# The last matrix product of a two-layer forward pass in wide groups with seven products for eight

## The chip, the cores and the metric

One core of a Trainium2 chip runs the kernel. The metric is the device time of one execution in microseconds: before, the median of 3 runs is 1776.52 us (1776.01 to 1777.11).

## The reference

256 tokens of width 2048 in float32 pass through two layers. The first is softmax attention with a forget-gate bias and a squared-ReLU MLP, each between norms. The second is a hybrid layer: a norm, one wide projection, block attention beside a gated spatial mix, two projections, and their gated sum. The change touches only its last line:

```python
    merged = jax.nn.sigmoid(g_a) * y_a + jax.nn.sigmoid(g_b) * y_b
    return x + merged @ w_out
```

`merged` is 256x2048 and `w_out` is 2048x2048.

## The kernel before

**Products.** Every float32 matrix is split into a high part (rounded to the type fp32r) and a low part (the rest), and a product of two blocks is three matmuls: high by high, low by high, high by low. A product here has 128 tokens (t = 0 or 1), a slice of 128 features of the input (kt, 0 to 15) and 512 output columns, and adds into one PSUM bank.

**The stream.** All weights come from one tensor `stream` in chunks of 128x1024 values. SP loads chunk c into slot c % 4 of `raw` (L393 to L395, and the loop at L432 to L436); it may do so once the low part of chunk c - 4 is made. ScalarE copies it to `w_hi` (L987, `split`/`next_split`), once TensorE is done with chunk c - 4 (`chunk_done`). VectorE makes `w_lo` = `raw` - `w_hi` (L1516, `rest`), which signals `lo_ready`, for which TensorE waits. `next_split(k)` and `rest(k, slot)` make the parts of chunk k + 4. Each engine runs its instructions in the order in which its block of the program lists them; that order is written by hand.

**Narrow groups.** The output phase (`FIRST["out"]`, 32 chunks) has four groups of 512 columns. A chunk of a narrow group holds two slices kt of its 512 columns, so 2 x 2 x 3 = 12 matmuls (`group_chunk`, L462). Groups alternate between two pairs of banks (2, 3 and 4, 5); at a group's end VectorE adds the residual rows to each bank (L2298) into `group_sum`, and SP stores that block (L441).

**Wide groups.** The MLP's second matrix and the q, k, v projection are done in groups of 1024 columns and 16 chunks. A chunk is one slice kt of 1024 columns: 2 token halves by 2 column blocks, 12 matmuls too (`wide_chunk`, L775). Three pairs of chunks (`SEVEN_AT`, chunks 4, 8 and 12, with the kt pairs 4, 5 and 6) are instead a 2x2 by 2x2 block product with seven products in place of eight, 21 matmuls (`seven_products`, L789; matmuls at L768 to L770). It needs:
- of x: four combinations of the four 128x128 blocks (`h_forms` on VectorE, L2041: two additions of high and low part, then four additions or subtractions), their high part on ScalarE (L1325) and low part on VectorE (`h_forms_lo`, L2064), once for all groups that share x
- of the weights, for each step: four 512-column additions or subtractions on VectorE (`outer_sums`, `inner_sum`, `last_sum`, L1866 to L1879), a 1536-column high part on ScalarE (`wide_form`, L1242) and low part on VectorE (`form_rest`, L1885)
- at the end: four banks of seven-products (`seven`) beside four banks of plain sums (`plain`). ScalarE copies `seven[0]` to SBUF (L1256), VectorE joins the others to it in four additions (`join_seven`, L1915 to L1924), and adds the plain banks in four more once the group is done (`plain_drain`, L1896).

One `wide_step` (VectorE) is: outer sums, inner sum, last sum, low part of two chunks, `form_rest`, low part of two chunks. In a group that follows another, the four drains of the group before are put between its sums.

**Around the output phase.** The projection `proj_a` has four groups. After its group n VectorE makes 512 columns of the merged matrix (L2276, L2282); TensorE turns them with eight transposes into banks 6 and 7 (`turn_merged`, L953) two to three chunks later; ScalarE makes the high part (`merged_to_hi`, L1491) and VectorE the low part (`merged_to_lo`, L2262), which counts `merged_ready` up by one for each kt, 16 in all. The last quarter, kt 12 to 15, is turned after the third chunk of the output phase. Before each chunk j of the first narrow group TensorE waits for `merged_ready` 2j + 2.

Of the kernel before, what the change touches and what calls it, by code (L numbers as in the profile page):

```python
# [43 lines left out]
QKV_WIDE = 3  # L44
EPS = 1e-6
# [52 lines left out]
def build(nc, stream, x, x_turned, fox_w_f, fox_b_f, norm_rows, norm_cols, w_spatial, b_spatial, head_cols, out):  # L98
    fox_scratch = nc.dram_tensor("cum_rows", (FOX_HEADS, TOK), F32, kind="Internal").ap()

    with ExitStack() as ctx:
# [90 lines left out]
        def in_a(name, at, shape, dt=F32R):  # L192
# [8 lines left out]
                          in_a("h_x_hi", 4608, [STEPS, 4, P]), in_a("h_x_lo", 6144, [STEPS, 4, P]), h_part)  # L201
        hidden = [gate_flat[:, b * 256:(b + 1) * 256] for b in range(2)]
# [22 lines left out]
        h_bank = [[bank[2], bank[3], bank[7], bank[6]], [bank[0], bank[1], bank[5], bank[4]]]  # L225
        h_seven = [[bank[0], bank[4], bank[1], bank[5]], [bank[2], bank[6], bank[3], bank[7]]]
# [165 lines left out]
        def _(sp):  # L392
# [44 lines left out]
            for n in range(4):  # L437
                for t in range(NT):
                    sp.wait_ge(out_ready, n * NT + t + 1)
                    cols_n = slice(n * GROUP_COLS, (n + 1) * GROUP_COLS)  # L440
                    sp.dma_start(out[0, t * P:(t + 1) * P, cols_n], group_sum[:, t, cols_n]).then_inc(stored, 16)  # L441
# [4 lines left out]
        def _(pe):  # L446
# [328 lines left out]
            def wide_chunk(c, j, kt, plain, x, bank_free={}):  # L775
# [3 lines left out]
                for t in range(NT):  # L779
                    for n in range(2):  # L780
                        if first and 2 * t + n in bank_free:
                            bank_free[2 * t + n]()
                        x_block = [part[:, kt, t * P:(t + 1) * P] for part in x]
                        mm = product(plain[2 * t + n], x_block, w_block(j % RING, n), first, last)
                    if last and t == 0:
                        mm.then_inc(half_group_done, 1)
# [185 lines left out]
            def merged_in(j):  # L972
                return lambda: pe.wait_ge(merged_ready, 2 * j + 2)
# [8 lines left out]
        def _(act):  # L982
# [261 lines left out]
            def wide_split(c, w, j, forms, seven):  # L1244
# [7 lines left out]
                if j == SEVEN_AT[-1] + 1:  # L1252
                    act.wait_ge(forms_done, STEPS * w + STEPS)
                    if 0 < w < WIDE_GROUPS:
                        act.wait_ge(added[0][0], 16 * w)
                    nc.scalar.activation(forms.part[0], seven[0][:, :], ACT.Copy).then_inc(form_hi_ready, 1)  # L1256
# [65 lines left out]
            def h_forms_hi(q):  # L1322

                act.wait_ge(x_form_step, 4 * STEPS * FF_GROUPS + 6 * q + 6)
# [187 lines left out]
        def _(dve):  # L1512
# [528 lines left out]
            def h_forms(q):  # L2041

                done = 4 * STEPS * FF_GROUPS + 6 * q
# [17 lines left out]
            def h_forms_lo(q):  # L2061

                dve.wait_ge(x_form_hi_ready, STEPS * FF_GROUPS + q + 1)
# [222 lines left out]
            for n in range(4):  # L2286
                cols_n = slice(n * GROUP_COLS, (n + 1) * GROUP_COLS)
                for j in range(8):
                    if 8 * n + j < 32 - RING:
                        rest(c + 8 * n + j, j % RING)  # L2290
                    if n == 0 and j == 2:
                        merged_to_lo(3)
                for t in range(NT):
                    if t == 0:
                        dve.wait_ge(half_group_done, GROUPS_BEFORE["out"] + n + 1)
                    else:
                        dve.wait_ge(chunk_done, c + 8 * n + 8)
# [253 lines left out]
```

## Time and profile before

| | us |
|---|---|
| median of 3 runs | 1776.52 |
| the profiled execution's own time | 1777.32 |
| its span in the trace | 1775.6 |
| TensorE busy | 1766.9 |
| VectorE busy | 1278.1 |
| ScalarE busy | 895.5 |

The trace is of one execution; its times count from the start of the span. PE is TensorE, DVE VectorE, ACT ScalarE. A line of a timeline merges like instructions that follow each other: start, time to the end of the last, how many. Matmuls overlap, so a matmul's own duration (0.39 us) is longer than the distance to the next.

### The profile page before, as it was taken

Reading aid. Unit: us, or ns where it says so; the run is one execution under the profiler, and the core shown is the slowest. Engines: PE = TensorE matmul, PEld = TensorE weight load, DVE = VectorE, ACT = ScalarE, POOL = GpSimd, SP = SyncE. Lnnn points to the kernel's source line nnn. Section 1 sums busy time; section 2 is a strip of 40 time slices with the busy share of each in tenths; the row PEclk is TensorE's granted clock in tenths of the full one; section 3 lists DMA queues with packets and bytes.
Section 4 is the critical chain, followed back from the end, with each engine's and each line's share of the span. In section 5 each row is a group of like instructions: output and inputs, shape, how many; then the busy total and the mean of one; then the engine's idle time right before and its main releaser. Section 6 shows DMA issues by size and latency. Waiting matters only on the chain.

```text
span 1775.6 us, 26289 instructions
## 1 busy us (share of the span) xinstructions
PE 1766.9 (100%) x8791; PEld 1496.7 (84%) x8791; DVE 1278.1 (72%) x1689; ACT 895.5 (50%) x1248; POOL 139.4 (8%) x190
## 2 busy tenths in 40 slices
PE   9999999999999999999999999999999999999999
PEld 7888888888888888888888887788888888888887
DVE  6567777556788788778887877899788655555654
ACT  7434444446456445545554455757644445553442
POOL 1012122000001000100000000010013011000000
PEclk9999999999999999999999999999999999999999
DMA  9664455555567666865785676566655655555554
GB/s 330 196 224 161 161 164 167 189 177 190 167 215 229 197 191 210 227 201 191 214 236 190 196 228 216 177 203 202 198 184 175 200 178 178 177 175 187 183 190 154
DMA packets 99116, 347.30 MB, mean 196 GB/s; under 512 B 11472, under 2 KB 11872, under 8 KB 98656
## 3 DMA queue, kind: packets, MB, share of 16 engines
q1 hardware_dynamic: 93392, 333.23, 57.3%
q0 software_dynamic: 4784, 12.60, 3.4%
q8 instruction: 50, 0.82, 0.2%
q10 hardware_dynamic: 864, 0.44, 0.1%
q14 instruction: 26, 0.21, 0.0%
HBM read 336.77 MB, written 2.11 MB: 191 GB/s over the span
## 4 chain that ended last, share of the span: by engine, by line
PE 94%; DVE 3%; ACT 1%; DMA 1%; issue 1%; POOL 0%; SPq 0%; ACTq 0%; DVEq 0%
PE bank L474 32%; PE bank L453 23%; PE bank L458 12%; PE bank L768 7%; PE bank L769 7%; PE bank L770 7%; PE bank L490 1%; PE bank L524 1%; DMA raw<-in_stream 1%; DVE w_lo L1516 1%; PE bank L603 1%; PE bank L646 1%; PE bank L661 1%; ACT w_hi L987 1%; PE bank L652 0%
## 5 line engine op out<-in xcount | busy, mean ns | idle before, releaser
L1516 DVE TENSOR_TENSOR w_lo<-raw,w_hi 128x1024 fp32r<-128x1024 f32 x620 | 753.9, 1224 | 372.1 <-ACT w_hi L987 368.1
L987 ACT ACTIVATE w_hi<-raw 128x1024 fp32r<-128x1024 f32 x620 | 648.3, 1055 | 583.8 <-PE bank L474 267.1
L453 PE MATMUL bank<-h_both,w_hi 128*128 128x512 f32 x1792 | 432.6, 393 | 0.0
L453 PEld LDWEIGHTS bank<-h_both,w_hi 128*128 128x128 f32 x1792 | 330.4, 188 | 65.4
L474 PE MATMUL bank<-w_hi,h_both 128*128 128x512 f32 x1160 | 361.6, 393 | 0.0
L474 PEld LDWEIGHTS bank<-w_hi,h_both 128*128 128x128 f32 x1160 | 215.8, 188 | 43.5
L458 PEld LDWEIGHTS bank<-h_both,w_lo 128*128 128x128 f32 x1792 | 229.8, 191 | 8.7
L458 PE MATMUL bank<-h_both,w_lo 128*128 128x256 f32 x1792 | 232.5, 283 | 0.0
L474 PE MATMUL bank<-w_lo,h_both 128*128 128x512 f32 x580 | 226.1, 390 | 0.0
L474 PE MATMUL bank<-w_hi,a_both 128*128 128x512 f32 x576 | 178.5, 391 | 0.0
L474 PEld LDWEIGHTS bank<-w_lo,h_both 128*128 128x128 f32 x580 | 108.9, 188 | 23.0
L474 PEld LDWEIGHTS bank<-w_hi,a_both 128*128 128x128 f32 x576 | 107.5, 188 | 21.9
L768 PE MATMUL bank<-w_hi,a_both 128*128 128x512 f32 x322 | 125.5, 390 | 0.2 <-DVE w_lo L1516 0.2
L769 PE MATMUL bank<-w_hi,a_both 128*128 128x512 f32 x322 | 125.3, 389 | 0.0
L770 PE MATMUL bank<-w_lo,a_both 128*128 128x512 f32 x322 | 125.3, 389 | 0.0
L474 PE MATMUL bank<-w_lo,a_both 128*128 128x512 f32 x288 | 112.2, 389 | 0.0
L1225 ACT ACTIVATE a_both<-gate 128x256 fp32r<-128x256 f32 (+1 forms) x56 | 23.4, 418 | 139.8 <-DVE gate L1818 139.8
L768 PEld LDWEIGHTS bank<-w_hi,a_both 128*128 128x128 f32 x322 | 60.5, 188 | 13.3 <-issue 0.8
L770 PEld LDWEIGHTS bank<-w_lo,a_both 128*128 128x128 f32 x322 | 60.4, 188 | 12.5
L769 PEld LDWEIGHTS bank<-w_hi,a_both 128*128 128x128 f32 x322 | 60.5, 188 | 12.3
L474 PEld LDWEIGHTS bank<-w_lo,a_both 128*128 128x128 f32 x288 | 54.1, 188 | 11.3
L2395 POOL DMA_DIRECT2D wide<-scaled x21 | 18.4, 1000 | 539.6 <-ACT scaled L1272 539.6
(278 smaller groups left out, 1784.9 us busy)
## 6 DMA issues: line engine op xcount, KB each, us to landing
raw<-in_stream SPq DMA_DIRECT2D x622, 512.0 KB, 3.5
wide<-scaled POOLq DMA_DIRECT2D x21, 256.0 KB, 4.7
res<-in_x SPq DMA_DIRECT2D x4, 512.0 KB, 7.1
rowg<-in_norm_rows POOLq DMA_DIRECT2D x2, 1024.0 KB, 8.3
gate<-cum_rows POOLq DMA_DIRECT2D x1, 2048.0 KB, 8.0
out<-wide SPq DMA_DIRECT2D x8, 256.0 KB, 3.6
wide<-gate POOLq DMA_DIRECT2D x7, 256.0 KB, 8.3
gate<-in_x_turned SPq DMA_DIRECT2D x5, 256.0 KB, 6.7
```

Of the source, the lines that this page charges most:

```text
L453: pe.matmul(tile_sum[b][:, :], w_hi[:, slot + half, k * P:(k + 1) * P], h_both[:, 8 * half + k, :], start=half == 0 and k == 0, stop=False)
L458: mm = pe.matmul(tile_sum[b][:, 0:TOK], w_lo[:, slot + half, k * P:(k + 1) * P], h_both[:, 8 * half + k, 0:TOK], start=False, stop=half == ...
L474: mm = pe.matmul(dst[t][:, :], xt[:, k0 + 2 * j + k, tt], wt[:, slot, w], start=j == 0 and k == 0 and n == 0, stop=last and k == 1 and n == 2)
L490: mm = pe.matmul(dst[t][:, :], xt[:, 2 * j + k, tt], wt[:, slot, w], start=j == 0 and k == 0 and n == 0, stop=j == GROUP_CHUNKS - 1 and k ...
L524: mm = pe.matmul(group_bank[0][t][:, :], xt[:, 2 * j + k, t * P:(t + 1) * P], wt[:, j % RING, w], start=first, stop=False)
L768: pe.matmul(dst[:, :], x_parts[0], w_parts[0], start=start, stop=False)
L769: pe.matmul(dst[:, :], x_parts[1], w_parts[0], start=False, stop=False)
L770: return pe.matmul(dst[:, :], x_parts[0], w_parts[1], start=False, stop=stop)
L987: nc.scalar.activation(w_hi[:, slot, :], raw[:, slot, :], ACT.Copy).then_inc(hi_ready, 1)
L1225: nc.scalar.activation(one(a_hi, i * 2 + b), relu2[b], ACT.Copy).then_inc(ff_hi, 1)
L1516: nc.vector.tensor_tensor(w_lo[:, slot, :], raw[:, slot, :], w_hi[:, slot, :].bitcast(F32), ALU.subtract).then_inc(lo_ready, 1)
L2395: pool.dma_start(group_sum[:, t, start:start + GROUP_COLS], src, accum_op=ALU.add).then_inc(added[t][n], 16)
```

## The change

The output phase becomes two wide groups of 1024 columns, each with three steps of seven products. The weights are laid out in the stream for that. It uses the forms' memory of the q, k, v phase (the weights' raw forms lie elsewhere). The forms of x are made again, of the merged matrix, at the start of the phase. The residual rows are added to the joined parts in SBUF (`add_rows`) and the drains add the plain banks. In the last chunk TensorE also signals when its third of four products is done, so that each drain of the second token half has its own signal, and the eight stores follow the drains.

```diff
+OUT_WIDE = 2
...
+        out_forms = qkv_forms._replace(w_raw=gate_flat[:, 6144:7680].rearrange("p (f n) -> p f n", f=3))
...
+        out_bank = [bank[2:6], [bank[0], bank[6], bank[7], bank[1]]]
+        out_seven = [[bank[0], bank[1], bank[6], bank[7]], [bank[2], bank[5], bank[3], bank[4]]]
...
-            pe.wait_ge(gate_taken[0], 9)
-            group_pair(FIRST["out"], 7, h_hi, h_lo, before={j: merged_in(j) for j in range(8)},
-                       after={2: lambda: turn_merged(3)})
-            group_pair(FIRST["out"] + 16, 8, h_hi, h_lo)
+            def out_group(i):
+
+                c = FIRST["out"] + 16 * i
+                w = WIDE_GROUPS + QKV_WIDE + i
+                if i:
+                    joined(w - 1)
+                else:
+                    pe.wait_ge(gate_taken[0], 9)
+                for j in range(0, WIDE_CHUNKS, 2):
+                    pair = PAIR_ORDER[j // 2]
+                    if i == 0:
+                        pe.wait_ge(merged_ready, 2 * pair + 2)
+                    if j in SEVEN_AT:
+                        if i:
+                            pe.wait_ge(out_ready, 4)
+                        else:
+                            pe.wait_ge(gate_taken[1], 9)
+                            pe.wait_ge(merged_ready, 16)
+                        seven_products(c, j, SEVEN_AT.index(j), w, out_bank[i], out_seven[i], (h_hi, h_lo), out_forms,
+                                       STEPS * (FF_GROUPS + 1))
+                        continue
+                    for k in range(2):
+                        wide_chunk(c, j + k, 2 * pair + k, out_bank[i], (h_hi, h_lo),
+                                   {3: fifth_read(w - 1)} if i else {}, i == OUT_WIDE - 1)
+                        if i == 0 and j + k == 2:
+                            turn_merged(3)
...
-            for k in range(32 - RING):
-                next_split(c + k)
-                if k == 2:
-                    merged_to_hi(3)
+            w = WIDE_GROUPS + QKV_WIDE
+            h_forms_hi(0, 1)
+            wide_split(c, w, 0, out_forms, out_seven[0])
+            h_forms_hi(1, 1)
+            wide_split(c, w, 1, out_forms, out_seven[0])
+            wide_split(c, w, 2, out_forms, out_seven[0])
+            merged_to_hi(3)
+            wide_split(c, w, 3, out_forms, out_seven[0])
+            h_forms_hi(2, 1)
+            for j in range(4, WIDE_CHUNKS):
+                wide_split(c, w, j, out_forms, out_seven[0])
+            for j in range(WIDE_CHUNKS - RING):
+                wide_split(c + 16, w + 1, j, out_forms, out_seven[1])
+            first_part(w + 1, out_forms, out_seven[1])
...
+            def add_rows(i):
+
+                dve.wait_ge(join_step, 8 * (w + i) + 4)
+                for block in range(4):
+                    t, n = divmod(block, 2)
+                    nc.vector.tensor_tensor(h_part[block], h_part[block], res[:, t, out_block(i, t, n)],
+                                            ALU.add).then_inc(join_step, 1)
...
+            step = STEPS * w
+            h_forms(0, 1)
+            outer_sums(step, c + 4, 0, out_forms)
+            inner_sum(step, 0, out_forms)
+            last_sum(step, 0, out_forms)
+            h_forms(1, 1)
+            rest(c, 0)
+            rest(c + 1, 1)
+            form_rest(step, out_forms)
+            h_forms_lo(0, 1)
+            h_forms_lo(1, 1)
+            rest(c + 2, 2)
+            merged_to_lo(3)
+            rest(c + 3, 3)
+            h_forms(2, 1)
+            wide_step(c, w, 1, out_forms)
+            h_forms_lo(2, 1)
+            wide_step(c, w, 2, out_forms)
+            rests(c + 12, range(2))
+            join_seven(w, out_seven[0], h_part)
+            rests(c + 12, range(2, RING))
+            add_rows(0)
+            for q in range(STEPS):
+                if q < STEPS - 1:
+                    wide_step(c + 16, w + 1, q, out_forms, (lambda t, n: out_drain(0, t, n)) if q == 0 else None)
+                else:
+                    outer_sums(step + 5, c + 28, 0, out_forms)
+                    inner_sum(step + 5, 0, out_forms)
+                    last_sum(step + 5, 0, out_forms)
+                    rests(c + 24, range(2))
+                    form_rest(step + 5, out_forms)
+                    rests(c + 24, range(2, RING))
+            join_seven(w + 1, out_seven[1], h_part)
+            add_rows(1)
+            for t in range(NT):
+                for n in range(2):
+                    out_drain(1, t, n)
```

`out_drain(i, t, n)` waits for its half group or last chunk and for its row addition, then writes `group_sum` = `h_part[block]` + bank and counts `out_ready` up; SP stores block by block on that count.

## Rows read from the trace of the kernel before

**Rows 1.** Page: busy time of each engine, and the slices' granted clock (tenths).
```profile
PE 1766.9 (100%) x8791; PEld 1496.7 (84%) x8791; DVE 1278.1 (72%) x1689; ACT 895.5 (50%) x1248; POOL 139.4 (8%) x190
...
PEclk9999999999999999999999999999999999999999
```

**Rows 2.** Chain that ended last, from 1600 us: start us, us, what.
```profile
1681.28 10.90 PE bank L474 x48
1692.18 0.87 PE bank L953 x8
1693.05 78.94 PE bank L474 x348
...
1772.02 0.69 DVE wide L2298
```

**Rows 3.** TensorE's waits: engine line <- releaser: us in total, times, longest.
```profile
PE bank L517 <- POOL ident L2309: 1.7, 1, 1.7
PE bank L768 <- DVE h_w_lo L1885: 1.3, 1, 1.3
```

**Rows 4.** Timeline of VectorE before the output phase: start us, us, engine, line, what.
```profile
1682.67 1.41 DVE L2262 SCALAR_TENSOR_TENSOR h_both<-bank,h_both 128x256 fp32r<-128x256 f32 x4
1685.14 1.23 DVE L1516 TENSOR_TENSOR w_lo<-raw,w_hi 128x1024 fp32r<-128x1024 f32 x1 [1.06 <-ACT w_hi L987]
1686.29 1.28 DVE L2276 SCALAR_TENSOR_TENSOR wide<-gate,bank 128x512 f32<-128x512 f32 x2
1687.71 1.29 DVE L2282 TENSOR_TENSOR wide<-wide 128x512 f32<-128x512 f32 x2
1688.92 1.22 DVE L1516 TENSOR_TENSOR w_lo<-raw,w_hi 128x1024 fp32r<-128x1024 f32 x1
```

**Rows 5.** Timeline of VectorE, forms of x in the q, k, v phase.
```profile
1123.45 1.06 DVE L2059 TENSOR_TENSOR gate<-gate 128x128 f32<-128x128 f32 x1
...
1125.57 0.75 DVE L2048 TENSOR_TENSOR gate<-h_both 128x256 f32<-128x256 f32 x2
...
1127.29 1.22 DVE L1516 TENSOR_TENSOR w_lo<-raw,w_hi 128x1024 fp32r<-128x1024 f32 x1
...
1131.68 1.89 DVE L2064 TENSOR_TENSOR h_x_lo<-gate,h_x_hi 128x512 fp32r<-128x512 f32 x3
```

**Rows 6.** Timeline of VectorE, third wide group of q, k, v.
```profile
1247.36 0.68 DVE L1866 TENSOR_TENSOR h_w_raw<-raw 128x512 f32<-128x512 f32 x1
...
1250.01 2.36 DVE L1516 TENSOR_TENSOR w_lo<-raw,w_hi 128x1024 fp32r<-128x1024 f32 x2
1252.28 1.75 DVE L1885 TENSOR_TENSOR h_w_lo<-h_w_raw,h_w_hi 128x1536 fp32r<-128x1536 f32 x1
1253.95 1.22 DVE L1516 TENSOR_TENSOR w_lo<-raw,w_hi 128x1024 fp32r<-128x1024 f32 x1
...
1260.71 0.69 DVE L1915 TENSOR_TENSOR gate<-gate,bank 128x512 f32<-128x512 f32 x1 [0.35 <-ACT gate L1256]
...
1262.76 0.68 DVE L1924 TENSOR_TENSOR gate<-gate,bank 128x512 f32<-128x512 f32 x1
...
1267.75 2.47 DVE L1896 TENSOR_TENSOR gate<-gate,bank 128x512 f32<-128x512 f32 x4
```

**Rows 7.** Timeline of ScalarE, the same group and the output phase.
```profile
1248.67 2.01 ACT L987 ACTIVATE w_hi<-raw 128x1024 fp32r<-128x1024 f32 x2 [1.11 <-DVE raw L1867]
1250.59 1.48 ACT L1242 ACTIVATE h_w_hi<-h_w_raw 128x1536 fp32r<-128x1536 f32 x1
...
1260.08 0.60 ACT L1256 ACTIVATE gate<-bank 128x512 f32<-128x512 f32 x1 [0.98 <-PE bank L770]
...
1693.18 1.19 ACT L1491 ACTIVATE h_both<-bank 128x256 fp32r<-128x256 f32 x4
```

**Rows 8.** Stores of the output (issues at L441): landing times.
```profile
DMA to landing us min/median/max: 2.4/3.6/5.3
```

**Rows 9.** Timeline of TensorE, the opening's transposes.
```profile
1.67 3.65 PE L517 MATMUL bank<-ident 128*128 128x128 f32 x19 [1.67 <-POOL ident L2309]
```

More of the change, by code:

```diff
@@ L436, in _ @@
                     load(j * RING + slot, slot)
-            for n in range(4):
+            for i in range(OUT_WIDE):
                 for t in range(NT):
-                    sp.wait_ge(out_ready, n * NT + t + 1)
-                    cols_n = slice(n * GROUP_COLS, (n + 1) * GROUP_COLS)
-                    sp.dma_start(out[0, t * P:(t + 1) * P, cols_n], group_sum[:, t, cols_n]).then_inc(stored, 16)
+                    for k in range(2):
+                        n = 2 * i + k
+                        sp.wait_ge(out_ready, 4 * i + 2 * t + k + 1)
+                        cols_n = slice(n * GROUP_COLS, (n + 1) * GROUP_COLS)
+                        sp.dma_start(out[0, t * P:(t + 1) * P, cols_n], group_sum[:, t, cols_n]).then_inc(stored, 16)
             sp.wait_ge(stored, 16 * 4 * NT)
@@ L784, in wide_chunk @@
                         mm = product(plain[2 * t + n], x_block, w_block(j % RING, n), first, last)
+                        if last and final and (t, n) == (1, 0):
+                            mm.then_inc(half_group_done, 1)
                     if last and t == 0:
@@ L1252, in wide_split, with first_part @@
                 if j == SEVEN_AT[-1] + 1:
[L1253 to L1256, printed above, removed]
+                    first_part(w, forms, seven)
+            def first_part(w, forms, seven):
+                act.wait_ge(forms_done, STEPS * w + STEPS)
+                if 0 < w < WIDE_GROUPS:
+                    act.wait_ge(added[0][0], 16 * w)
+                if w == WIDE_GROUPS + QKV_WIDE + 1:
+                    act.wait_ge(out_ready, 4)
+                nc.scalar.activation(forms.part[0], seven[0][:, :], ACT.Copy).then_inc(form_hi_ready, 1)
             def wide_splits(g, n):
@@ L2040, in _, with h_forms @@
             c = FIRST["qkv"]
-            def h_forms(q):
-                done = 4 * STEPS * FF_GROUPS + 6 * q
+            def h_forms(q, lap=0):
+                done = 4 * STEPS * FF_GROUPS + 6 * (STEPS * lap + q)
+                if lap:
+                    dve.wait_ge(merged_ready, 2 * SEVEN_PAIRS[q] + 2)
                 if q:
@@ L2285, in _ @@
             c = FIRST["out"]
[L2286 to L2297, printed above, removed]
-                    nc.vector.tensor_tensor(group_sum[:, t, cols_n], group_bank[n % 2][t][:, :],
-                                            res[:, t, cols_n], ALU.add).then_inc(out_ready, 1)
-                dve.wait_ge(out_ready, 2 * n + 2)
-                dve.sem_inc(group_taken[n % 2], 1)
+            w = WIDE_GROUPS + QKV_WIDE
@@ new lines, in out_block @@
+            def out_block(i, t, n):
+                start = i * 1024 + n * GROUP_COLS
+                return slice(start, start + GROUP_COLS)
+            def add_rows(i):
[4 more added lines that the diff above has]
+                                            ALU.add).then_inc(join_step, 1)
@@ new lines, in out_drain @@
+            def out_drain(i, t, n):
+                block = 2 * t + n
+                if t == 0:
+                    dve.wait_ge(half_group_done, GROUPS_BEFORE["out"] + i + 1)
+                elif i == 1 and n == 0:
+                    dve.wait_ge(half_group_done, GROUPS_BEFORE["out"] + 3)
+                else:
+                    dve.wait_ge(chunk_done, c + 16 * i + WIDE_CHUNKS)
+                dve.wait_ge(join_step, 8 * (w + i) + block + 5)
+                nc.vector.tensor_tensor(group_sum[:, t, out_block(i, t, n)], h_part[block], out_bank[i][block][:, :],
+                                        ALU.add).then_inc(out_ready, 1)
```

19 lines of the change are left out of this document (11 added, 8 removed).

## The prediction

> **What bounds the kernel now.** I read the page first: TensorE is busy for the whole span and the granted clock stands at 9 or more in every slice [rows 1]. The chain of waits says the same of the end: one run of matmuls, with eight transposes between, reaches 1771.99 us, then one VectorE addition of 0.69 us and the last store [rows 2]. The list of TensorE's waits is led by a 1.7 us start and one wait of 1.3 us [rows 3]. So a product less is time less, as long as TensorE stays fed, and any wait put on TensorE is time more. 348 matmuls take 78.94 us [rows 2], 0.227 us each; 12 of them, one chunk, 2.72 us. The output phase starts 36 matmuls and 8.2 us before 1692.18, about 1684.0. About 0.2% (3.6 us) is what a measurement of this kernel can tell from no change.
>
> **Products removed.** Each of two groups has three steps in which 21 matmuls replace 24: 18 fewer, 18 x 0.227 = **-4.1 us**. The stream's bytes and the transposes stay as they are.
>
> **A new wait at the start of the phase.** The first step (chunks 4 and 5) writes banks 0, 1, 6 and 7. Banks 6 and 7 hold the turned last quarter of the merged matrix until VectorE has made its low part, so TensorE waits for merged_ready 16 there. Before, only the eighth chunk of the phase needed that count. TensorE reaches the step after chunk 3, at 1693.05 + 2.72 = 1695.8. I walk VectorE's queue up to the instruction it waits for. VectorE ends the last merging additions at about 1688.9, when it starts the next low part now [rows 4]. In the changed order it then has, by starts of consecutive rows:
> - two sums and four combinations of pair 4: 1127.29 - 1125.57 = 1.72 [rows 5]
> - four weight combinations: 1250.01 - 1247.36 = 2.65 [rows 6]
> - the same six for pair 5: 1.72
> - low parts of chunks 4 and 5: 2 x 1.14, from 2.27 for two [rows 6]
> - the low part of the three weight forms: 1.67 [rows 6]
> - two low parts of the x forms: 1.2, from 1.89 for three [rows 5]
> - low part of chunk 6: 1.14
> - the four low parts of the merged quarter: 1.41 [rows 4].
>
> That is 13.8 us. ScalarE adds to it, because its queue too is in order: the high part of chunk 5 stands behind the high part of pair 5's form, which waits for VectorE until 1694.9, so at 1.0 us for a chunk (2.01 for two [rows 7]) VectorE idles 0.6; the three forms' high part (1.48) follows, another 0.2. ScalarE's four high parts of the quarter (1.19 [rows 7]) are done near 1700.0 and hold nobody. Sum 14.6: VectorE delivers at 1703.5, and TensorE stands for about **7.8 us** (+7.8, counted from its last matmul's issue, 0.1 more than from its modelled end). All of it is bare, since nothing else runs on TensorE. Bounds: 7.0 without ScalarE's part, 9.0 with one stumble such as the 1.06 us that one 128-column combination took where the others took 0.28 [rows 5].
>
> **The rest of the phase.** TensorE has 318 matmuls left, 72.1 us, so its end would be 1703.5 + 72.1 = 1775.6 by issue, 1775.8 by modelled end. VectorE must keep up with twice its old load. Per group: 16 low parts (18.2), three times four combinations and a form (13.0), four joins (2.7), four row additions (2.4), four drains (2.4), 38.7 us against TensorE's 8 x 5.44 - 3 x 0.68 = 41.5. The first group adds 2.3 for pair 6. Walked in order, VectorE's form for the third step is done at 1723.5 for a need at 1726.6, and that of the second group's first step at 1747.9 for a need at 1747.7: a wait of 0.1 or 0.2. The projection of q, k and v runs the same steps, and its one wait was 1.3 us at the phase's first step [rows 3]. I take 0, bounds 0 and 1.3. SP's stream loads are issued when a low part is done, so they go late with VectorE; the four-slot ring leaves 3 us or more between landing and use in my walk, so 0.
>
> **Row additions and tail.** The residual rows leave the last drain and become four additions of their own, after the join. No row shows one; the nearest is an SBUF-only addition of the same size, 1.29 us for two [rows 4], and a drain that reads PSUM, 2.47 for four [rows 6]: 0.60 to 0.65 each. In group 0 they are hidden behind TensorE. In the last group they are not. The last step ends 24 matmuls before the end, at 1770.4; ScalarE's copy takes 0.60 [rows 7], to 1771.0; the four joins 2.7 [rows 6], to 1773.7; four row additions 2.4, to 1776.1; four drains, all behind them in the queue, 2.5, to 1778.6. So VectorE ends 2.8 us behind TensorE where it now ends 0.7 behind: **+2.1**, bounds 1.6 and 3.0. If the row additions were on another engine, the drains would end at about 1776.5 and the tail cost nothing.
>
> **Stores.** The same eight stores, but the last four now come 0.6 us apart instead of the last two six matmuls (1.4 us) apart. Now 2.9 us pass from the last addition to the span's end; landings are 2.4 to 5.3 [rows 8]. I take **+0.2**, bounds 0 and 1.0.
>
> **The clock after the stand.** Nothing in this trace idles TensorE for more than 1.7 us [rows 3], so no row shows what 7.8 us do. The nearest is the opening: TensorE comes out of idle and makes 19 transposes in 3.65 us, 0.192 each [rows 9], where eight of the same size later take 0.87, 0.109 each [rows 2]. By that pace it started at the lower level, 1.2 GHz. That cost 19 x 0.083 = 1.6 us. After a stand four times as long as any here I expect the same, and 512-column products lose more each than transposes do: I take **+2.0**, bounds 0 (the rival below) and 3.2, twice the opening.
>
> A row and a page part here. The granted clock reads full in every slice, the opening too [rows 1], though the transposes there run slow; by that row alone the sum would lack the 2.0. The Trainium skill, "TensorE: Matmul & The Clock Gate", section "Why this matters for your kernels", says that idle gaps between bursts of matmuls put the clock back to its lower level; by it the sum keeps a clock term. No run here shows that yet.
>
> **Sum.** -4.1 + 7.8 + 0 + 2.1 + 0.2 + 2.0 = +8.0 us on the profiled execution (span 1775.6, time 1777.32, which is 0.8 above the median). A difference carries over: 1776.52 + 8.0 = **1784.5**.
>
> **Rivals.**
> 1. *The stand without the clock.* TensorE stays at the upper level; 1784.5 - 2.0 = 1782.5. For it: the granted clock never moves in this trace. Against: the slow transposes of the opening.
> 2. *VectorE becomes the bound after the stand as well.* It starts the rest late and has some 81 us of work in the 90 us from 1688.9 to its end; if three of the five remaining steps each wait 1.3 us, as the one in the q, k, v phase [rows 3], 3.9 more: 1788.4. Against: that phase ran two whole groups with the same queue and no wait, though without the row additions.
> 3. *Not slower: the stand does not form.* The place is the wait for merged_ready 16 at chunk 4. If VectorE came to the quarter's low part before 1695.8, 7.8 and 2.0 fall away: 1774.7, 0.1% under before and within what can't be told. It decides at 1.8 us: a shorter stand gives a gain, a longer one a loss (-4.1 + 2.1 + 0.2 = -1.8). Against it: that low part is behind 12 us of VectorE work which can't begin before 1688.9. For it only that I have misread the order of a queue. That the products are not saved can't be: their number is fixed in the code.
>
> **Chances.** Forecast 0.62, rival 1 0.24, rival 2 0.07, rival 3 0.07. The range: low end with the stand at 7.0, the tail at 1.8 and no clock term, -4.1 + 7.0 + 1.8 + 0.1 = 4.8, 1781.3; high end with the clock at 3.2, tail and stand a little long, near 1788.0. It leaves out rivals 2 and 3 and little more. Faster by over 0.2% needs rival 3 and a hidden tail: 0.02. Within 0.2%: the rest of rival 3 and a little: 0.06. Slower: 0.92.
>
> **What would show it.** In the changed profile TensorE's waits should have one long entry near 1695, about 7.8 us, released by VectorE's low part of the merged quarter (the scalar_tensor_tensor from the bank), and VectorE in one block from 1688.9 to 1703.5 with two small gaps left by ScalarE. Instructions: 18 matmuls fewer. Matmul starts just after the stand should be about 0.43 us apart (512 columns at 1.2 GHz) rather than 0.227 if the clock fell; with rival 1 they are 0.227 at once. At the end VectorE should run 12 additions without a gap of note and finish 2.8 us after the last matmul. The forecast is wrong if the stand is under 5 us or absent, if later steps wait more than 1.5 us in all, or if the tail is as short as now.

## The result, and the profile after

| | us |
|---|---|
| before, median of 5 (1776.01 to 1777.11) | 1776.52 |
| after, median of 5 (1785.96 to 1787.08) | 1786.66 |
| forecast | 1784.5 (1781.3 to 1788.0) |

The ratio is 1.0056 (95% interval 1.0045 to 1.0068): 10.1 us slower, where 8.0 were forecast. The profiled execution has a span of 1785.4 us against 1775.6, a difference of 9.8, and that is what the rows below add up to.

The page's first lines and its row of granted clock:

```profile
span 1785.4 us, 26353 instructions
...
PE 1765.9 (99%) x8773; PEld 1495.9 (84%) x8773; DVE 1318.3 (74%) x1756; ACT 906.3 (51%) x1259; POOL 140.6 (8%) x190
...
PEclk9999999999999999999999999999999999999989
```

18 matmuls fewer than in [rows 1], as the code says, and one dent in the row of nines: the 39th of 40 slices, 1696 to 1741 us, in which the output phase starts. A slice is 44.6 us long and a 9 stands for 90% or more, so this row shows 10 us at half the clock and would hide 3 us. TensorE's waits (engine, line <- releaser: us in total, times, longest):

```profile
PE bank L774 <- DVE h_both L2310: 8.0, 1, 8.0
PE bank L523 <- POOL ident L2406: 1.7, 1, 1.7
PE bank L774 <- DVE h_w_lo L1931: 1.4, 1, 1.4
```

The last two stood there before [rows 3]. The first is new, alone, and 8.0 us long; what released it is the low part of the merged quarter. VectorE's timeline shows the queue that the prediction walked:

```profile
1687.29 1.30 DVE L2330 TENSOR_TENSOR wide<-wide 128x512 f32<-128x512 f32 x2
1688.51 0.75 DVE L2096 TENSOR_TENSOR gate<-h_both 128x256 f32<-128x256 f32 x2
...
1690.23 0.68 DVE L1912 TENSOR_TENSOR gate<-raw 128x512 f32<-128x512 f32 x1
...
1692.89 0.75 DVE L2096 TENSOR_TENSOR gate<-h_both 128x256 f32<-128x256 f32 x2
...
1694.61 1.22 DVE L1562 TENSOR_TENSOR w_lo<-raw,w_hi 128x1024 fp32r<-128x1024 f32 x1
1696.34 1.23 DVE L1562 TENSOR_TENSOR w_lo<-raw,w_hi 128x1024 fp32r<-128x1024 f32 x1 [0.51 <-ACT w_hi L1017]
1697.71 1.76 DVE L1931 TENSOR_TENSOR h_w_lo<-gate,h_w_hi 128x1536 fp32r<-128x1536 f32 x1
1699.39 1.28 DVE L2112 TENSOR_TENSOR h_x_lo<-gate,h_x_hi 128x512 fp32r<-128x512 f32 x2
1700.59 1.22 DVE L1562 TENSOR_TENSOR w_lo<-raw,w_hi 128x1024 fp32r<-128x1024 f32 x1
1701.72 1.41 DVE L2310 SCALAR_TENSOR_TENSOR h_both<-bank,h_both 128x256 fp32r<-128x256 f32 x4
```

From the merging additions (1687.29, 0.4 us earlier than in [rows 4]) to the quarter's low part at 1701.72 there is one gap, 0.51 us at chunk 5, behind ScalarE, and 0.2 more before 1697.71. TensorE over the same time, its last matmul before and the first after the stand:

```profile
1695.02 0.39 PE L776 MATMUL bank<-w_lo,h_both 128*128 128x512 f32 x1
1703.39 0.76 PE L774 MATMUL bank<-w_hi,h_both 128*128 128x512 f32 x1 [7.99 <-DVE h_both L2310]
1703.95 0.63 PE L775 MATMUL bank<-w_hi,h_both 128*128 128x512 f32 x1
1704.38 0.63 PE L776 MATMUL bank<-w_lo,h_both 128*128 128x512 f32 x1
...
1708.64 0.47 PE L774 MATMUL bank<-h_w_hi,h_x_hi 128*128 128x512 f32 x1
1708.95 0.40 PE L775 MATMUL bank<-h_w_hi,h_x_lo 128*128 128x512 f32 x1
```

The first interval is 0.56 us, the eleven behind it are 0.43 each, the last, from 1708.64, is 0.31; then the products are 0.23 apart again. The windows of the timeline give the granted clock beside it (columns: the stretch, its length, busy time and count of TensorE's matmuls, of its weight loads, of VectorE, ScalarE and GpSimd, then the granted clock, the DMA share and GB/s):

```profile
1684.00:1695.00 11.00, 11.00 (x54) 9.17 (x53) 9.92 (x22) 2.66 (x4) 0.00 (x0) 1.00 0.22 82
1695.00:1703.00 8.00, 0.40 (x2) 0.00 (x0) 7.34 (x10) 5.66 (x9) 0.00 (x0) 0.72 0.38 131
1703.00:1709.00 6.00, 5.61 (x14) 4.43 (x15) 5.86 (x13) 1.80 (x3) 0.00 (x0) 0.52 0.53 178
1709.00:1715.00 6.00, 6.00 (x28) 4.98 (x27) 3.98 (x4) 3.50 (x3) 0.00 (x0) 1.00 0.48 175
```

0.52 from 1703 to 1709: TensorE runs at 1.2 GHz, the lower of its two levels. It had stood idle since 1695.4 (the last matmul before, 1695.02 + 0.39); from 1709 on it is back at 2.4 GHz (1.00). The end, VectorE:

```profile
1769.32 2.35 DVE L1562 TENSOR_TENSOR w_lo<-raw,w_hi 128x1024 fp32r<-128x1024 f32 x2
1773.72 0.69 DVE L1961 TENSOR_TENSOR gate<-gate,bank 128x512 f32<-128x512 f32 x1 [2.06 <-ACT gate L1292]
...
1776.49 2.50 DVE L2346 TENSOR_TENSOR gate<-gate,res 128x512 f32<-128x512 f32 x4
1778.90 2.47 DVE L2359 TENSOR_TENSOR wide<-gate,bank 128x512 f32<-128x512 f32 x4
```

and TensorE's last matmul:

```profile
1778.11 0.39 PE L776 MATMUL bank<-w_lo,h_both 128*128 128x512 f32 x1
```

TensorE ends at 1778.11 + 0.39 = 1778.50. VectorE waits for ScalarE's copy until 1773.72 and then has twelve additions without a pause, to 1778.90 + 2.47 = 1781.37, which is 2.87 behind TensorE; before it was 0.7 [rows 2]. From there to the end of the span are 4.0 us, before 2.9.

So the difference of the spans, in microseconds, by rows:

| | forecast | measured |
|---|---|---|
| the stream up to the output phase | 0 | -0.4 |
| 18 products | -4.1 | -4.1 |
| the stand at chunk 4 | +7.8 | +8.0 |
| 13 slow intervals after the stand: 1708.95 - 1703.39 = 5.56, less 13 x 0.227 | +2.0 | +2.6 |
| the rest of the phase | 0 | +0.4 |
| VectorE behind TensorE at the end | +2.1 | +2.1 |
| from the last addition to the end | +0.2 | +1.1 |
| sum | +8.0 | +9.8 (rounded terms give 9.7) |

The -4.1 is the count times the price of one product, as in the forecast; no row measures it alone. The 0.4 in the rest of the phase is what is left when TensorE's end, 6.5 us later than before, is set against the other terms. By the distances of its matmuls, 0.15 of it lies at the edge of the stand (8.14 us of extra distance for 7.99 in the brackets). The prediction counted its 7.8 from the last matmul's issue, which is the 8.14; by that way of counting the rest of the phase is 0.2. That 0.2 lies at 1747.3 to 1747.6, at the first step of group 1, where I had foreseen 0.1 to 0.2 and took none.

### The profile page after: what moved, and what is told of

It is laid out like the page before. It is cut to its first block, busy times and chain, and to the rows that moved or that the text cites. A ratio compares the mean times of both kernels' runs of the same rounds, so it can differ in the third digit from the quotient of the medians.

```text
span 1785.4 us, 26353 instructions
## 1 busy us (share of the span) xinstructions
PE 1765.9 (99%) x8773; PEld 1495.9 (84%) x8773; DVE 1318.3 (74%) x1756; ACT 906.3 (51%) x1259; POOL 140.6 (8%) x190
## 4 chain that ended last, share of the span: by engine, by line
PE 93%; DVE 3%; ACT 2%; issue 1%; DMA 1%; POOL 0%; DVEq 0%; ACTq 0%; SPq 0%; POOLq 0%
PE bank L480 25%; PE bank L459 23%; PE bank L464 12%; PE bank L774 9%; PE bank L776 9%; PE bank L775 9%; PE bank L530 1%; PE bank L496 1%; DVE w_lo L1562 1%; ACT w_hi L1017 1%; DMA raw<-in_stream 1%; PE bank L609 1%; PE bank L652 1%; PE bank L667 1%; PE bank L658 0%
## 5 line engine op out<-in xcount | busy, mean ns | idle before, releaser
L480 PE MATMUL bank<-w_hi,h_both 128*128 128x512 f32 x904 | 282.6, 394 | 0.0
L480 PEld LDWEIGHTS bank<-w_hi,h_both 128*128 128x128 f32 x904 | 167.8, 188 | 33.6
L480 PE MATMUL bank<-w_lo,h_both 128*128 128x512 f32 x452 | 176.3, 390 | 0.0
L480 PEld LDWEIGHTS bank<-w_hi,a_both 128*128 128x128 f32 x576 | 107.4, 188 | 22.4 <-DVE w_lo L1562 0.6
L480 PEld LDWEIGHTS bank<-w_lo,h_both 128*128 128x128 f32 x452 | 84.8, 188 | 18.0
L774 PE MATMUL bank<-w_hi,h_both 128*128 128x512 f32 x230 | 90.4, 393 | 8.4 <-DVE h_both L2310 8.0
L776 PE MATMUL bank<-w_lo,h_both 128*128 128x512 f32 x230 | 90.0, 391 | 0.0
L775 PE MATMUL bank<-w_hi,h_both 128*128 128x512 f32 x230 | 90.0, 391 | 0.0
L774 PEld LDWEIGHTS bank<-w_hi,a_both 128*128 128x128 f32 x322 | 60.4, 188 | 12.7 <-issue 0.3
L776 PEld LDWEIGHTS bank<-w_lo,a_both 128*128 128x128 f32 x322 | 60.5, 188 | 12.6
```

Of the source, the lines that this page charges most:

```text
L480: mm = pe.matmul(dst[t][:, :], xt[:, k0 + 2 * j + k, tt], wt[:, slot, w], start=j == 0 and k == 0 and n == 0, stop=last and k == 1 and n == 2)
L774: pe.matmul(dst[:, :], x_parts[0], w_parts[0], start=start, stop=False)
L775: pe.matmul(dst[:, :], x_parts[1], w_parts[0], start=False, stop=False)
L776: return pe.matmul(dst[:, :], x_parts[0], w_parts[1], start=False, stop=stop)
```

## The experiments

My theory: four separate costs, each with its own place (VectorE's queue at chunk 4; the clock that falls during that stand; VectorE's queue behind the last step; the stores), against 4.1 us of saved products. The rivals: the step itself makes TensorE slow; VectorE's added work is too much wherever it is put; the stores alone set the end.

One table for all kernels helps to read what follows. "TensorE's part" is from the start of the last eight transposes (1692.02 before) to the last matmul's start; "VectorE behind" is the end of the last addition less the end of the last matmul; "stores" from there to the end of the span. The kernel before was run again beside each batch of experiments; its row gives the range of its medians.

| kernel | time, median | TensorE's part | VectorE behind | stores |
|---|---|---|---|---|
| before | 1776.52 to 1776.72 | 79.57 | 0.7 | 2.9 |
| after | 1786.66 | 86.51 | 2.9 | 4.0 |
| e1_fill | 1784.27 | 83.89 | 2.9 | 4.0 |
| e2_norows | 1784.65 | 85.88 | 1.15 | 4.0 |
| e3_order | 1780.73 | 80.39 | 2.9 | 4.0 |
| e4_five_steps | 1778.97 | 78.76 | 2.9 | 4.0 |
| e5_five_reordered | 1777.09 | 76.65 | 2.9 | 4.0 |
| e6_four_steps | 1775.76 | 77.33 | 1.2 | 4.0 |
| e7_two_queues | 1786.17 | 86.80 | 2.9 | 4.0 |
| e8_four_steps_blocks | 1774.30 | 77.30 | 0.7 | 2.9 |
| e9_no_steps | 1776.49 | 79.57 | 0.7 | 2.9 |

**e1_fill: is it the idle time that makes the products slow?**

```diff
                             pe.wait_ge(gate_taken[1], 9)
+                            for _ in range(33 if j == 4 else 0):
+                                pe.matmul(bank[0][:, :], h_hi[:, 0, 0:P], h_both[:, 0, :], start=True, stop=True)
                             pe.wait_ge(merged_ready, 16)
```

> The changed kernel, with 33 dummy matmuls of 512 columns (7.5 us) into the still unused bank 0 ahead of TensorE's wait for merged_ready 16; nothing of the real work is changed. My theory: the 12 products after the stand run 0.427 us apart because TensorE was idle before them, at the lower of its two levels. With the dummies there is no idle time, the products are 0.227 apart at once, the granted clock stays at 1.00, and the time falls by 12.5 x 0.2 = 2.5 us: 1784.2 us; the wait's end stays where it is. Rival: the slow products come from the step itself (its operands, or VectorE and ScalarE at the same memory); then the same 12 products stay slow and the time stays at 1786.7.

1784.27 us, 2.4 less than the changed kernel. The same windows as above, of this kernel:

```profile
1695.00:1703.00 8.00, 7.68 (x34) 6.05 (x34) 7.33 (x11) 5.25 (x8) 0.00 (x0) 1.00 0.46 144
1703.00:1709.00 6.00, 6.00 (x27) 4.95 (x27) 5.86 (x12) 2.81 (x4) 0.00 (x0) 1.00 0.45 160
```

TensorE is busy through the stand, the granted clock stays at 1.00, and 27 matmuls fit where 14 did. TensorE's part is 2.6 shorter, the amount of the clock term. More work made the kernel faster: the term is the idle time's, not the step's, and rival 1 of the prediction (no fall of the clock) is out.

**e2_norows: the row additions in the tail.**

```diff
             join_seven(w + 1, out_seven[1], h_part)
-            add_rows(1)
+            dve.wait_ge(join_step, 8 * (w + 1) + 4)
+            dve.sem_inc(join_step, 4)
```

> The changed kernel without the four row additions of the second group, so that the residual rows are missing from the right half of the output; group 0 is unchanged. My theory: the end is VectorE's queue of 12 additions behind the last step. Four fewer, 2.4 us, but then the drains wait for TensorE's last products, whose end is 0.7 us before the last drain's: VectorE ends about 1.6 us earlier, 1785.0 us. Rival: the stores set the end (four stores close together, 4.0 us from the last addition to the end of the span where before had 2.9): the drains then come as close together as now, and the time falls by under 0.7 us.

1784.65 us, 2.0 less; 1.6 expected. VectorE's last two rows:

```profile
1774.76 0.68 DVE L1970 TENSOR_TENSOR gate<-gate,bank 128x512 f32<-128x512 f32 x1
1776.16 2.48 DVE L2359 TENSOR_TENSOR wide<-gate,bank 128x512 f32<-128x512 f32 x4 [0.72 <-PE bank L776]
```

The drains now wait 0.72 us for TensorE, and end 1.15 behind it in place of 2.87: 1.7 us for the row additions. TensorE's part is 0.6 shorter as well: in this execution only the first eight products after the stand were 0.43 us apart, where the changed kernel's profile had twelve. That made the clock term 1.9 us here; in the profile of e7, with the same stand, it is 2.9. So that term is not the same in every execution. The stores still take 4.0 us, so the row additions have no part in that.

**e3_order: the same work in another order.**

```diff
...
-            h_forms(1, 1)
-            rest(c, 0)
-            rest(c + 1, 1)
-            form_rest(step, out_forms)
             h_forms_lo(0, 1)
-            h_forms_lo(1, 1)
-            rest(c + 2, 2)
+            rest(c, 0)
             merged_to_lo(3)
+            rest(c + 1, 1)
+            form_rest(step, out_forms)
+            rest(c + 2, 2)
             rest(c + 3, 3)
-            h_forms(2, 1)
+            h_forms(1, 1)
+            h_forms_lo(1, 1)
             wide_step(c, w, 1, out_forms)
+            h_forms(2, 1)
             h_forms_lo(2, 1)
             wide_step(c, w, 2, out_forms)
```

(ScalarE's queue follows it.)

> The changed kernel with another order at the start of the output phase: VectorE makes first what the first step needs (forms of pair 4, its weight forms, low part of chunk 4, low part of the merged quarter, low part of chunk 5, the weight forms' low part), and the forms of pairs 5 and 6 right before their own steps; ScalarE's queue is put in the same order. All 18 products stay saved. My theory: the stand of 8.0 us is the order and the sum of VectorE's work. By the rows, the quarter's low part is then done at 1695.4 instead of 1703.1 and the weight forms at 1699.7: the first step costs some 1.6 us of waits in three pieces, the second about 2, the third about 1, no piece long enough for the clock: 4.5 us of waits in place of 8.0 + 2.5, so 1780.7 us. Rival: VectorE is short of time for the whole of group 0 and the waits come back at the later steps almost in full, 7 us or more: 1783 us or over.

1780.73 us, as expected to the tenth. TensorE's timeline at the starts of the three steps of group 0 (the time it sat idle before stands in brackets):

```profile
1696.87 0.47 PE L774 MATMUL bank<-w_hi,h_both 128*128 128x512 f32 x1 [0.89 <-DVE h_both L2311]
...
1708.74 0.47 PE L774 MATMUL bank<-w_hi,h_both 128*128 128x512 f32 x1 [1.39 <-DVE w_lo L1563]
...
1720.72 0.47 PE L774 MATMUL bank<-w_hi,h_both 128*128 128x512 f32 x1 [1.50 <-DVE w_lo L1563]
```

and the windows over them:

```profile
1696.00:1704.00 8.00, 7.13 (x31) 5.93 (x32) 7.34 (x12) 3.05 (x4) 0.00 (x0) 1.00 0.68 205
1704.00:1712.00 8.00, 6.61 (x29) 5.12 (x28) 7.83 (x9) 5.35 (x6) 0.00 (x0) 1.00 0.42 141
1712.00:1730.00 18.00, 16.50 (x73) 13.26 (x72) 16.92 (x23) 9.58 (x10) 0.00 (x0) 1.00 0.63 210
```

There is a wait at every step now, 0.9 to 1.5 us, 3.8 in the brackets and 4.9 by TensorE's part (80.39, where 79.57 less 4.1 for the products would be 75.5), and the granted clock is 1.00 throughout: short pieces cost a little more than their own length, and no clock. VectorE really lacks time in group 0 (the rival's premise), but under 5 us of it, not 7. So about half of the 8.0 us was order, and with it went the whole clock term; the other half is VectorE's work, which comes back in pieces. The first interval after such a wait is 0.31 us at the full clock too, so 0.1 of the changed kernel's 2.6 belongs to the restart and not to the clock.

**e4_five_steps: the first step plain.** The step at chunk 4 of group 0 is left to plain products (`OUT_STEPS`), its counters are advanced by hand, and the start of the phase is put in another order (the first weight sums and their low part are gone).

```diff
+OUT_STEPS = ((1, 2), (0, 1, 2))
...
-                    if j in SEVEN_AT:
+                    if j in SEVEN_AT and SEVEN_AT.index(j) in qs:
...
+            act.sem_inc(form_hi_ready, 1)
+            next_split(c)
             h_forms_hi(0, 1)
-            wide_split(c, w, 0, out_forms, out_seven[0])
+            next_split(c + 1)
             h_forms_hi(1, 1)
...
+            rest(c, 0)
             h_forms(0, 1)
+            rest(c + 1, 1)
             h_forms(1, 1)
+            rest(c + 2, 2)
             h_forms_lo(0, 1)
             h_forms_lo(1, 1)
             merged_to_lo(3)
             rest(c + 3, 3)
+            wide_step(c, w, 1, out_forms)
             h_forms(2, 1)
```

> The changed kernel with the first step of group 0 (chunks 4 and 5) computed plainly, with eight products: five steps in all. Chunk 4 no longer needs forms or banks 6 and 7, and VectorE makes the low parts of chunks 4 to 7, the merged quarter and the forms of x between TensorE's first eight chunks. My theory: no wait of over 1 us in the phase, no loss of clock, 3 products more: 1786.7 - 8.0 - 2.5 + 0.7 = 1776.9 us, the time of before, because the tail still costs 3.1 of the 3.4 that five steps save. Rival: VectorE's added work (20 us of forms and sums) holds TensorE somewhere in group 0 whatever the first step is; then over 1779.

1778.97 us: 2.1 over the expectation, just under the rival's bound. The stand is gone, but TensorE still waits 1.50 us at chunk 12:

```profile
1718.13 0.47 PE L775 MATMUL bank<-w_hi,h_both 128*128 128x512 f32 x1 [1.50 <-DVE w_lo L1568]
```

VectorE's timeline shows why it is late:

```profile
1692.72 1.23 DVE L1568 TENSOR_TENSOR w_lo<-raw,w_hi 128x1024 fp32r<-128x1024 f32 x1 [1.65 <-ACT w_hi L1021]
...
1697.33 1.23 DVE L1568 TENSOR_TENSOR w_lo<-raw,w_hi 128x1024 fp32r<-128x1024 f32 x1 [1.65 <-ACT w_hi L1021]
```

Two gaps of 1.65 us. ScalarE's queue had the high part of a form of x, which needs VectorE, ahead of the high part of chunk 5 (and 6), which VectorE then needed: each engine stood in line behind the other. That is my order's fault, so the run does not tell the two theories apart.

**e5_five_reordered: the two gaps removed.**

```diff
             next_split(c)
-            h_forms_hi(0, 1)
             next_split(c + 1)
-            h_forms_hi(1, 1)
+            h_forms_hi(0, 1)
             next_split(c + 2)
+            h_forms_hi(1, 1)
             merged_to_hi(3)
             next_split(c + 3)
+            h_forms_hi(2, 1)
```

(On VectorE the forms of pair 6 come before the first weight sums, and the low part of pair 4's form before that of chunk 6.)

> The five-step kernel (first step of group 0 plain) with the start of the phase in another order: ScalarE makes the high parts of chunks 4 and 5 before it waits for the first form of x, and the forms of x of all three pairs are made before the first weight sums. My theory: the five-step kernel's 1.5 us wait at chunk 12, with 0.24 at chunk 8, came from two gaps of 1.65 us that VectorE spent behind ScalarE near 1691 and 1696, not from VectorE's total work; without them VectorE is 2 us or more ahead at chunk 8, both waits are gone and the time is 1779.0 - 1.8 = 1777.2 us, which is the time of before: five steps save 3.4, the tail gives them back. Rival: VectorE's sum of work bounds group 0; then a wait of over 1 us stays at chunk 12 and the time is over 1778.5.

1777.09 us, expected 1777.2; the ratio to before is 1.0003 (0.9994 to 1.0012). From TensorE's list of waits:

```profile
PE bank L524 <- POOL ident L2409: 1.7, 1, 1.7
PE bank L775 <- DVE h_w_lo L1936: 1.4, 1, 1.4
...
PE bank L775 <- DVE w_lo L1567: 0.4, 1, 0.4
```

The first two are those of the kernel before [rows 3], and the third, too, lies in the q, k, v phase; none is in the output phase. So VectorE's work is not too much for group 0 when one step fewer is asked at its start. TensorE's part is 2.9 us shorter than before, of the 3.4 that fifteen products are worth, and the tail (2.2) and the stores (1.1) eat that.

**e6_four_steps: the last step plain as well.** The join and the row additions of group 1 fall into TensorE's last four chunks.

```diff
-OUT_STEPS = ((1, 2), (0, 1, 2))
+OUT_STEPS = ((1, 2), (0, 1))
...
+            rests(c + 24, range(2))
+            join_seven(w + 1, out_seven[1], h_part, 2)
+            rests(c + 24, range(2, RING))
             add_rows(1)
```

(ScalarE's copy of `seven[0]` moves up in the same way.)

> As the reordered five-step kernel, and the last step of group 1 (chunks 12 and 13) plain as well: four steps, 12 products saved in place of 18. The join and the row additions of group 1 then run while TensorE still has four chunks to do. My theory: the tail of 2.1 us and most of the 1.1 us at the stores go, 0.7 us of products come back: 1777.2 - 2.1 - 0.8 + 0.7 = 1775.0 us, below the 1776.6 of before. VectorE ends one drain (0.7 us) behind TensorE. Rival: the stores set the end whatever VectorE does, since four of them still fall into the last 2 us; then 1776.2 or more.

1775.76 us, 1.3 less than e5 where 2.2 were expected; the ratio to before is 0.9995 (0.9986 to 1.0004), no gain that can be told. VectorE's last row:

```profile
1767.49 2.48 DVE L2368 TENSOR_TENSOR wide<-gate,bank 128x512 f32<-128x512 f32 x4 [4.79 <-PE bank L777]
```

It now waits for TensorE (4.79 us), yet the four drains follow each other without a pause: three of the four banks are finished within the last 1.4 us, so VectorE ends 1.2 behind, and the stores take 4.0 as before. Half of the expectation failed: the stores don't care for the join. That it is their closeness was the theory left; e8 tests it.

**e7_two_queues: who issues the stores.** This is the changed kernel with six steps again; ScalarE issues the last two stores, and SP skips them.

```diff
+            for k in range(2):
+                act.wait_ge(out_ready, 7 + k)
+                cols_n = slice((2 + k) * GROUP_COLS, (3 + k) * GROUP_COLS)
+                act.dma_start(out[0, P:2 * P, cols_n], group_sum[:, 1, cols_n]).then_inc(stored, 16)
```

> The changed kernel with the last two of its eight stores issued by ScalarE instead of SP. From the last addition to the span's end it takes 4.0 us in every kernel with four close drains, 2.9 before. My theory: four transfers of 256 KB within 1.8 us share the DMA engines, so that it doesn't matter who issues them: the time stays at 1786.7 within 0.5. Rival: SP's queue hands them on one after the other; with two queues the end comes about 1 us earlier, 1785.6.

1786.17 us, 0.5 less, which lies halfway between the two expectations and can't be told from no change (its ratio to before is 1.0053, 1.0038 to 1.0068, against 1.0056). The profile decides: there are still 4.0 us from the last addition to the end, and the two stores that ScalarE issues take 3.5 and 3.6 us from issue to landing, as the last two of the changed kernel do. SP's queue is not the cause.

**e8_four_steps_blocks: the same products as e6, the banks finished apart.**

```diff
+                    if i == OUT_WIDE - 1 and j == WIDE_CHUNKS - 2:
...
+                        for block in range(4):
+                            t, n = divmod(block, 2)
+                            for k in range(2):
+                                x_block = [part[:, 2 * pair + k, t * P:(t + 1) * P] for part in (h_hi, h_lo)]
+                                mm = product(out_bank[i][block], x_block, w_block((j + k) % RING, n), False, k == 1)
+                            mm.then_inc((chunk_done, half_group_done, half_group_done, chunk_done)[block], 1)
```

(VectorE's first drain waits for the first of these signals.)

> The four-step kernel with the last two chunks of group 1 taken block by block: TensorE does both chunks for one token half and column block (six products) before it goes to the next, so that the four banks are finished 1.36 us apart and not three of them within the last 1.4 us. No product more or less. My theory: in the four-step kernel VectorE still ended 1.2 us behind TensorE and the end of the span came 4.0 us after the last addition, because four drains and stores fell together; now VectorE ends 0.7 behind and the stores are as far apart as in the kernel before, whose gap was 2.9: 1775.8 - 0.5 - 1.1 = 1774.2 us. Rival: the 4.0 us belong to the number of stores or to the wide layout, not to their distance; then 1775.3.

1774.30 us, expected 1774.2; the ratio to before is 0.9986 (0.9977 to 0.9995). VectorE's end:

```profile
1764.79 0.69 DVE L2380 TENSOR_TENSOR wide<-gate,bank 128x512 f32<-128x512 f32 x1 [0.68 <-PE bank L777]
...
1768.87 0.69 DVE L2380 TENSOR_TENSOR wide<-gate,bank 128x512 f32<-128x512 f32 x1 [0.67 <-PE bank L777]
```

Drains 1.36 us apart, the last 0.7 behind TensorE, and 2.9 us from there to the end of the span. TensorE's part is the same as e6's (77.30 and 77.33), so all of the 1.5 us came from the order of the last 24 products. This version beats both kernels, the one before by 0.14%.

The traces also show what the distance does. Here are the DMA engines' busy share (tenths) and GB/s in 40 slices each of 1780 to 1785 us in the changed kernel (0.125 us a slice) and of 1766 to 1772 us in this one (0.15 us), with the times from issue to landing of the last four stores of each. The changed kernel's three lines come first:

```profile
DMA  0003999999998999999999989979897461000000
GB/s 0 0 0 131 426 360 377 360 426 361 360 360 246 360 393 426 197 229 213 279 229 213 213 164 279 246 148 262 262 311 230 164 131 33 0 0 0 0 0 0
DMA to landing us min/median/max: 2.6/3.3/3.6
...
DMA  0079998100068998100049998100039999100000
GB/s 0 0 273 369 369 396 314 28 0 0 0 246 341 410 382 328 41 0 0 0 177 396 396 410 328 41 0 0 0 137 410 410 396 341 55 0 0 0 0 0
DMA to landing us min/median/max: 2.4/2.5/2.5
```

With banks 1.36 us apart each store is through (about 0.8 us of busy engines, at up to 410 GB/s) before the next begins. With drains 0.60 us apart the engines are busy in one block, and from the middle of it they move only 150 to 310 GB/s. The last store then takes 3.6 us to land in place of 2.5, which is the 1.1 us. So the stores share the DMA engines, as e7's theory said; why the rate falls in the second half, these runs don't tell.

**e9_no_steps: e8 without seven products.**

```diff
-OUT_STEPS = ((1, 2), (0, 1))
+OUT_STEPS = ((), ())
...
-                nc.vector.tensor_tensor(group_sum[:, t, out_block(i, t, n)], h_part[block], out_bank[i][block][:, :],
+                nc.vector.tensor_tensor(group_sum[:, t, out_block(i, t, n)], out_bank[i][block][:, :],
+                                        res[:, t, out_block(i, t, n)], ALU.add).then_inc(out_ready, 1)
```

> As the kernel of the run before this one, with no step of seven products at all: two wide groups of 16 plain chunks, no forms, no join, residual rows added in the drains from the banks. It has the 12 products back that four steps save. My theory: they cost 12 x 0.227 = 2.7 us and nothing else changes: 1776.9 us, the time of before. Rival: the forms' work on VectorE and ScalarE slows TensorE or the stream by something the waits don't show; then the difference of the two kernels is under 2 us.

1776.49 us, and TensorE's part is 79.57, that of the kernel before to the hundredth. Against it four steps bring 2.2 us in the medians and 2.27 in TensorE's part, where 12 products are 2.7. So the wide layout is free, and the steps lose 0.45 of their 2.7 us: 0.3 in gaps under 0.15 us each between matmuls around the starts of steps, too short for the list of waits; the rest is not located. The difference of 2.2 lies above the rival's 2, but the rival is right in kind for those 0.45 us.

## Why the prediction was right

- **Products.** -4.1 by count, as forecast; e9 against e8 gives 2.27 for 12 of them in place of 2.7, so four steps keep five sixths of the price.
- **The new wait.** Right in place, releaser and size. The stand is 8.0 us by the brackets and 8.14 by the prediction's own way of counting, for 7.8; VectorE's queue took 13.9 us for 13.8 and ScalarE added 0.7 for 0.8. Both ends came earlier than forecast (TensorE reached the wait at 1695.2 in place of 1695.8, VectorE delivered at 1703.1 in place of 1703.5), which leaves the difference nearly as it was. Rival 3 (no stand) is out. e3 and e5 show that the stand is the order and the amount of VectorE's early work: TensorE's part falls by 6.1 with another order and the same products, 2.6 of it the clock, and the stand vanishes with one step fewer.
- **The rest of the phase.** I took 0 within bounds of 0 and 1.3; it was 0.4. Rival 2 (VectorE the bound all along) did not come about in the changed kernel. It is the state of e3, where the waits were spread over the steps of group 0. That the long stand gave VectorE the time to keep up is my reading of the two.
- **The tail.** +2.1 forecast, +2.1 measured; e2 gives 1.7 of it to the row additions, and e8 removes all of it.
- **The stores.** This term was mis-sized: +0.2 taken, +1.1 measured, just beyond my upper bound of 1.0. I read a landing time per store and did not ask what four stores do to each other, though [rows 8] held a hint: in that trace the last two stores, 1.4 us apart, landed 2.4 and 2.5 us after their issue, and the six before them, closer together and beside the stream's loads, after 3.4 to 5.3. It is their distance: 4.0 us in every kernel with drains 0.60 us apart, 2.9 in the three whose last drains are 1.36 apart.
- **The clock.** The term was right in kind: e1 takes away the idle time alone and gains 2.4. Its size was partly luck. I read the opening as 19 transposes at a mean of 0.192 us. In fact they are of two kinds:

```profile
1.67 2.99 PE L517 MATMUL bank<-ident 128*128 128x128 f32 x13 [1.67 <-POOL ident L2309]
...
4.50 0.49 PE L517 MATMUL bank<-ident 128*128 128x128 f32 x3
```

Thirteen start from 1.67 to 4.29, 0.22 us apart, and from 4.50 on the others are 0.11 apart. So the opening lost 13 x 0.11 = 1.4 us, not 1.6. From there I went to 2.0 by a guess. Three profiles of the same stand gave 1.9 (e2), 2.6 (the changed kernel) and 2.9 (e7), all within my bounds of 0 and 3.2.

I also said that the granted clock reads full in the opening. The row can't bear that. A 9 in a slice of 44 us would hide 3 us at half the clock; and the trace has no record of the clock before 4.49 us, just where the transposes become fast, and the views count time without a record as 1.00. After the stand there is a record, and the granted clock is 0.52. The Trainium skill, "TensorE: Matmul & The Clock Gate", section "Why this matters for your kernels", says that idle gaps between bursts of matmuls put the clock back to its lower level. The trace agrees, with 0.52 after the 8.0 us. The sum without the clock (1782.5) would have missed by 4.2 us.

With the stores at 1.1, the clock at 2.6, the rest at 0.4 and the stand at 8.0 the sum is 10.1, the measured difference of the medians; the profiled executions differ by 0.4 us less, because the stream ahead of the phase was that much quicker in the changed kernel's. The three terms that missed all missed to the same side, so no error hid another.

## What to carry to other kernels

When work is added to a side engine, walk that engine's queue from the moment it can start to the instruction on which the bound engine waits; the average load (VectorE was at 74% of the span) says nothing of that place. If a stand of many microseconds can't be avoided, split it into short ones or do a piece of work the plain way: here one step less at the start, one less at the end, and the last 24 products taken block by block turned a loss of 10.1 us into a gain of 2.4. The two steps alone brought it to within the noise of before (e6). At the end of a kernel, finish the last banks one after the other, so that the drains and stores don't fall together.

## What the hardware showed that I had not expected

- Four stores of 256 KB issued 0.6 us apart ended 4.0 us after the last addition, in eight kernels, whether one queue or two issued them; four issued 1.36 us apart ended after 2.9, in two. The close ones keep the DMA engines busy in one block, and these move mostly 360 to 430 GB/s in its first half and 150 to 310 in its second.
- Waits of 0.9, 1.4 and 1.5 us within 25 us left the granted clock at 1.00; one of 8.0 us brought it to 0.5, and the number of products 0.43 us apart behind it differed between executions: twelve in the changed kernel, eight in e2, thirteen in e7.
- In the opening the granted clock reads 1.00 because the trace has no record of it before 4.49 us. The transposes' own distances show what the column hides: 0.22 us up to 4.50, then 0.11.
